# Expert blocks re-cut: rooms of 160 to 32 tokens by rank, 46 blocks of up to three experts, additions without the empty places, further blocks tested in sevens

## What is computed

```python
scores = sigmoid(uf @ w_router)              # 512 tokens, 64 experts
choice = scores + router_bias
masked = where(expert in the 4 best of 8 groups, choice, -inf)
_, top_e = top_k(masked, 8)                  # 8 experts of each token: 4096 rows in all
wts = scores[top_e] / sum(scores[top_e]) * 2.5
for each expert e:                           # D_MODEL 1024, D_EXPERT 256
    hid = silu(xb @ we_gate[e]) * (xb @ we_up[e])     # xb: the tokens that chose e
    routed[token] += (hid @ we_down[e]) * weight
shared = (silu(uf @ ws_gate) * (uf @ ws_up)) @ ws_down
return routed + shared
```

## Time and profile before

| what | value |
|---|---|
| time, median of 3 runs | 3088.01 us (3082.47 to 3090.04) |
| profiled execution: its own time | 3083.99 us |
| profiled execution: span of the core | 3082.7 us |
| PE busy | 2765.7 us, 90% of the span |
| DVE / ACT / POOL busy | 35% / 23% / 5% |
| TensorE clock granted, mean | 0.951 of full |
| DMA moved | 434.28 MB, mean 141 GB/s |

### The profile page before, as it was taken

One profiled execution on the slowest core, in us unless ns is written; L12 is line 12 of the kernel. 1 busy time (PEld: TensorE's weight loads), 2 busy tenths in 40 slices (PEclk: granted clock), 3 DMA queues, 4 the chain that ended last, 5 costly groups with the idle time before them and its releaser, 6 DMA issues.

```text
span 3082.7 us, 40644 instructions
## 1 busy us (share of the span) xinstructions
PE 2765.7 (90%) x16440; PEld 1663.5 (54%) x16440; DVE 1076.4 (35%) x2331; ACT 718.6 (23%) x1176; POOL 164.6 (5%) x132
## 2 busy tenths in 40 slices
PE   5999997999989799999999479979996988999797
PEld 2666663444437566677676234427875433555443
DVE  7666664322212122222222131016774113333312
ACT  2333331100021111111111020134553212333311
POOL 0000000000000122222222000000000000000000
PEclk8999998999998899999999789989998999999899
DMA  6222111333313598999999513221111211111110
GB/s 238 107 85 82 69 65 44 123 136 123 136 59 138 195 332 286 386 376 374 373 368 362 166 48 121 79 109 41 44 48 48 101 68 36 55 55 55 34 41 27
DMA packets 79045, 434.28 MB, mean 141 GB/s; under 512 B 11888, under 2 KB 12272, under 8 KB 36240
## 3 DMA queue, kind: packets, MB, share of 16 engines
q1 hardware_dynamic: 53296, 366.37, 30.7%
q0 software_dynamic: 15872, 46.16, 6.4%
q10 hardware_dynamic: 9696, 19.18, 1.7%
HBM read 395.95 MB, written 46.20 MB: 143 GB/s over the span
## 4 chain that ended last, share of the span: by engine, by line
PE 78%; DVE 8%; DMA 7%; ACT 5%; issue 2%; SPq 0%; DVEq 0%; POOL 0%; ACTq 0%; POOLq 0%
PE psum_all L274 34%; PE psum_all L1411 10%; PE psum_all L1853 7%; PE psum_all L1458 5%; DMA weights<-t_experts 4%; PE psum_all L3247 4%; PE psum_all L2000 4%; PE psum_all L3120 3%; PE psum_all L284 3%; PE psum_all L299 1%; PE psum_all L629 1%; DVE big L3381 1%; DVE h L3168 1%; DMA h<-x_t 1%; DMA total_rows<-big,rows 1%
## 5 line engine op out<-in xcount | busy, mean ns | idle before, releaser
L274 PE MATMUL psum_all<-u,weights 128*128 128x512 f32 x1024 | 449.8, 596 | 12.2 <-issue 12.2
L274 PE MATMUL psum_all<-big,weights 128*128 128x512 f32 (+1 forms) x768 | 338.1, 595 | 6.7 <-DVE big L3413 4.2
L274 PEld LDWEIGHTS psum_all<-u,weights 128*128 128x128 f32 x1024 | 193.8, 191 | 246.1 <-issue 245.7
L1411 PE MATMUL psum_all<-big 128*128 128x256 f32 (+1 forms) x1280 | 261.5, 383 | 15.4 <-ACT big L1390 15.4
L274 PEld LDWEIGHTS psum_all<-big,weights 128*128 128x128 f32 (+1 forms) x768 | 144.5, 189 | 194.4 <-issue 187.8
L1411 PEld LDWEIGHTS psum_all<-big 128*128 128x128 f32 (+1 forms) x1280 | 210.7, 180 | 53.6 <-ACT big L1390 16.0
L1853 PE MATMUL psum_all<-big,weights 128*128 128x512 f32 x512 | 222.3, 597 | 14.0 <-DVE big L1923 14.0
L1853 PEld LDWEIGHTS psum_all<-big,weights 128*128 128x128 f32 x512 | 98.1, 192 | 138.2 <-issue 134.2
L274 PE MATMUL psum_all<-weights,u 128*128 128x256 f32 (+1 forms) x704 | 153.5, 383 | 9.6 <-ACT u L412 9.6
L274 PEld LDWEIGHTS psum_all<-weights,u 128*128 128x128 f32 x704 | 135.2, 203 | 30.3 <-ACT u L412 10.4
L284 PE MATMUL psum_all<-const_cols,big 128*128 128x128 f32 (+2 forms) x952 | 133.3, 280 | 18.6 <-DVE big L789 11.0
(11 more groups left out here) (346 smaller groups left out, 3394.8 us busy)
## 6 DMA issues: line engine op xcount, KB each, us to landing
big<-t_experts SPq DMA_DIRECT2D x96, 1024.0 KB, 23.2
weights<-t_experts SPq DMA_DIRECT2D x96, 1024.0 KB, 18.0
weights<-t_ada SPq DMA_DIRECT2D x24, 1024.0 KB, 7.0
weights<-t_rkvg SPq DMA_DIRECT2D x16, 1024.0 KB, 5.5
rwkv_inputs<-big ACTq DMA_DIRECT2D x48, 256.0 KB, 2.0
big<-rwkv_inputs SPq DMA_DIRECT2D x8, 1280.0 KB, 6.8
weights<-t_x SPq DMA_DIRECT2D x8, 1024.0 KB, 4.9
weights<-t_BC SPq DMA_DIRECT2D x8, 1024.0 KB, 4.9
```

What stands on the lines that cost most here:

```text
L274: last = pe.matmul(out, lhsT, rhs, start=n == 0, stop=n == len(terms) - 1)
L1411: ins = pe.matmul(K.psum[rows, bank, n * F_E:(n + 1) * F_E], xT[:, k, rows], X.part(r, n, KD, F_E)[:, k, :], start=k == 0, stop=k == KD - 1)
```

## The change

**Rooms and blocks.** Rooms are now 160 (ranks 0 to 7), 128 (8 to 23), 96 (24 to 31), 64 (32 to 55) and 32 (56 to 63), which is enough for the counts given above. The 46 blocks are of four kinds: 24 `alone` (one expert, 128 places), 10 `two` (64 and 64), 8 `most` (96 places of one of the ranks 24 to 31 and 32 of one of 56 to 63) and 4 `more` (places 128 to 159 of two of the ranks 0 to 7, 32 partitions each, and 64 places of one of 32 to 35). `ORDER`, the order of the loads, follows from the first use of each rank.

**Matmuls.** `shares` cuts a part of 96 places into 64 and 32, so `most` and `more` blocks take three matmuls for each column of weights where a block of two took two. The list of a block comes from one group of matmuls, without the second one of two columns.

**Additions.** Each part of a block has an addition of its own, over all 128 places, in which the places outside the part and the empty ones carry a number over 511 and are left out. There are 24 + 10 x 2 + 8 x 2 + 4 x 3 = 72 additions; before there were 32 + 20 x 2 = 72. Real rows are 4096; before, 32 x 128 + 40 x 64 = 6656 rows were added, 2560 of them to spare rows.

**Start.** The shared output goes to four buffers of its own, in the room of u, so no copy waits for a store, and POOL issues the stores ahead of most gathers.

**Further blocks.** The loop is nested: five tests, and only if one holds, seven turns behind it.

```diff
+ROOM = [160] * 8 + [128] * 16 + [96] * 8 + [64] * 24 + [32] * 8
+SPANS = ((0, 128), (0, 96), (96, 128), (0, 64), (64, 128), (0, 32), (32, 64))
...
-    put("spare_row", T + r + 0 * c[:, 0:2])
+    put("spare_row", np.concatenate([T + np.where((r >= a) & (r < b), r, 4 * T) for a, b in SPANS], 1))
...
-    for j in range(16):
-        yield (2 * j,), 0
-        yield (2 * j + 1,), 0
-        if 2 * j < WITH_MORE:
-            yield (2 * j, 2 * j + 1), P
-        yield (ALONE + 2 * j, ALONE + 2 * j + 1), 0
+    alone = lambda r: [(r, 0, 0, 128)]
+    two = lambda r, s: [(r, 0, 0, 64), (s, 0, 64, 128)]
+    most = lambda r, s: [(r, 0, 0, 96), (s, 0, 96, 128)]
+    more = lambda r, s, t: [(r, 128, 0, 32), (s, 128, 32, 64), (t, 0, 64, 128)]
+    for j in range(4):
+        yield from (alone(2 * j), alone(2 * j + 1), more(2 * j, 2 * j + 1, 32 + j))
+        yield from (most(24 + 2 * j, 56 + 2 * j), alone(8 + 4 * j), two(36 + 5 * j, 37 + 5 * j), alone(9 + 4 * j))
+        yield from (most(25 + 2 * j, 57 + 2 * j), alone(10 + 4 * j), two(38 + 5 * j, 39 + 5 * j), alone(11 + 4 * j))
+        if j % 2:
+            yield two(35 + 5 * j, 40 + 5 * j)
...
-    ins = products(pe, K.psum[:, 7, 0:4], [(X.sel[n][:, t, :], X.rhs[n][:, t, :]) for t in range(NT)])
-    if two:
-        ins = products(pe, K.psum[0:HEAD, 7, 4:6], [(X.sel[n][:, t, HEAD:P], X.rhs[n][:, t, 0:2]) for t in range(NT)])
-    ins.then_inc(*q.pe.tick("list", b))
+    products(pe, K.psum[:, 7, 0:m], [(X.sel[n][:, t, :], X.rhs[n][:, t, 0:m]) for t in range(NT)]).then_inc(*q.pe.tick("list", b))
...
+    for r, _, start, end in BLOCKS[b]:
+        if end - start == 96:
+            yield r, slice(start, start + 64)
+            yield r, slice(start + 64, end)
+        else:
+            yield r, slice(start, end)
...
-    if len(BLOCKS[e][0]) == 1:
-        pool.indirect_dma_start(K.total_rows, bass.IndirectOffsetOnAxis(ap=rows[:, 1:2], axis=0), y, None,
-                                compute_op=ALU.add).then_inc(*K.added.tick(e))
-        return
...
+    if len(parts) > 1:
+        pool.wait_ge(*q.dve.at("add lists", e))
+    for i in range(len(parts)):
+        n = 1 if len(parts) == 1 else 2 + i
+        pool.indirect_dma_start(K.total_rows, bass.IndirectOffsetOnAxis(ap=rows[:, n:n + 1], axis=0), y, None,
+                                bounds_check=T - 1, oob_is_err=False, compute_op=ALU.add) \
+            .then_inc(*(K.added.tick(e) if i == len(parts) - 1 else K.added.tick(e, i)))
+        if i < len(parts) - 1:
+            pool.wait_ge(*K.added.at(e, i))
...
-            if t >= 2 and half == 0:
-                act.wait_ge(*K.shared_stored[t % 2].at(t - 2))
-            act.activation(X.y[t % 2][:, half * 512:half * 512 + 512], K.psum[:, 2 * (t % 2) + half, :], ACT.Copy) \
+            act.activation(X.shared_y[t][:, half * 512:half * 512 + 512], K.psum[:, 2 * (t % 2) + half, :], ACT.Copy) \
...
-    with nc.Fori(0, EXTRA) as i:
-        with nc.If(i < limit):
+    with nc.Fori(0, EXTRA, SEVEN) as first:
+        with nc.If(first < limit):
+            with nc.Fori(0, SEVEN) as n:
+                i = first + n
```

More of the change, by code:

```diff
@@ L1047, in __init__ @@
         self.sel = [K.carve(NT, P) for _ in range(2)]
-        self.rhs = [K.carve(NT, 4) for _ in range(2)]
+        self.rhs = [K.carve(NT, 6) for _ in range(2)]
         self.info = [K.carve(8) for _ in range(self.TURN)]
@@ L1056, in __init__ @@
         self.y = [K.carve(D) for _ in range(2)]
+        self.shared_y = [K.u[:, 2 * t:2 * t + 2, :].rearrange("p a b -> p (a b)") for t in range(NT)]
         self.ring = [K.carve(2048) for _ in range(6)] + [slot[:, :] for slot in K.W.slots]
@@ L1317, in select_dve @@
 def select_dve(K, X, q, b):
-    dve, n, (ranks, first) = K.nc.vector, b % 2, BLOCKS[b]
-    m = P // len(ranks)
+    dve, n, parts = K.nc.vector, b % 2, BLOCKS[b]
     if b >= 2:
@@ L1347, in list_dve @@
     dve.wait_ge(*q.pe.at("list", b))
[L1348 removed]
+    dve.tensor_copy(info[:, 0:2 + len(parts)], K.psum[:, 7, 0:2 + len(parts)]).then_inc(*q.dve.tick("rows", b))
     dve.wait_ge(*q.dve.now())
     dve.scalar_tensor_tensor(info[:, 6:7], info[:, 1:2], X.minus, info[:, 0:1], ALU.mult, ALU.add).then_inc(*q.dve.tick())
[L1351 to L1354 removed]
+    for i, (_, _, start, end) in enumerate(parts[1:]):
+        dve.tensor_copy(info[start:end, 2:3], info[start:end, 3 + i:4 + i]).then_inc(*q.dve.tick())
     dve.wait_ge(*q.dve.now())
[L1356 to L1358 removed]
+    dve.tensor_tensor(rows[:, 1:2], info[:, 6:7], K.c("spare_row")[:, 0:1], ALU.add).then_inc(*q.dve.tick("gather list", b))
+    if len(parts) > 1:
+        for i, (_, _, start, end) in enumerate(parts):
+            n = SPANS.index((start, end))
+            dve.tensor_tensor(rows[:, 2 + i:3 + i], info[:, 6:7], K.c("spare_row")[:, n:n + 1], ALU.add) \
+                .then_inc(*(q.dve.tick("add lists", b) if i == len(parts) - 1 else q.dve.tick()))
 def gather_pool(K, X, q, b):
@@ L1367, in gather_pool @@
         pool.wait_ge(*q.pe.at("turn", b - X.AHEAD, 1))
-    pool.wait_ge(*q.dve.at("listed", b))
+    pool.wait_ge(*q.dve.at("gather list", b))
     pool.indirect_dma_start(X.x_rows[b % X.AHEAD], None, K.u_rows,
@@ L1483, in add_pool @@
 def add_pool(K, X, q, e):
-    pool = K.nc.gpsimd
+    pool, y, rows, parts = K.nc.gpsimd, X.y[e % 2], K.rows[e % X.TURN], BLOCKS[e]
     if e:
@@ L3601, in build_program @@
     K.u_stored, K.added = K.new_signal("u_stored"), K.new_signal("rows_added")
-    K.shared_stored = [K.new_signal(f"shared_stored{n}") for n in range(2)]
+    K.shared_stored = K.new_signal("shared_stored")
     K.gathered = [K.new_signal(f"gathered{n}") for n in range(Moe.AHEAD)]
@@ L3611, in build_program @@
     K.expert_in = [K.new_signal(f"expert_in{n}") for n in range(Moe.RING)]
-    K.rows = [K.sb(f"rows{n}", [P, 3], I32) for n in range(Moe.TURN)]
+    K.rows = [K.sb(f"rows{n}", [P, 5], I32) for n in range(Moe.TURN)]
     K.number = K.sb("numbers", [P, 2 + E_ALL], I32)
```

66 lines of the change are left out of this document (23 added, 43 removed).

## The result

The changed kernel takes 3202.5 us (median of 4 runs, 3195.66 to 3206.07), the kernel before 3086.47 us on the same chip: a ratio of 1.0376, 95% interval 1.0361 to 1.039. The forecast was 3065 us with a range of 3036 to 3095, so the change cost 116 us where it was to gain some 20. The profiled execution has a span of 3204.8 us.

A forecast was written before the change was run, and what follows sets the result against it. PE, the loads and the chain of additions were taken to be at their limit together. From 3084.0 us, 20 less for loads, 12 more for additions and 12.5 less for the loop gave 3063.5, raised to 3065; range 3036 to 3095.

The forecast's parts named there:

- the part on PE: PE's products: 46 rounds of 12.57 us instead of 52 of about 13, 98 us less; three-part blocks at price 0.
- two at a time: Gate and up of three-part blocks: if parts overlapped only so, 3.6 us more in 12 blocks, 43 us; 0 was taken.
- the three-part blocks at 10 us and more: Gate and up of `most` and `more` blocks: a sign that the forecast is wrong; it expected 7.1 us.
- The start: First gate product: some 1008.4 instead of 1021.7 us, 13.2 us earlier; the loads decide what of it lasts.
- The loop: Tests after the last addition: 26 fewer save 12.5 us, 14.4 at most, at 0.48 us each.
- The bytes: Additions on q0: 2560 empty places dropped save 10.5 MB, and a load falls from 3.39 to 3.3 us.
- The price of 10.2 us: Chain of additions: a part naming 128 places lasts between a half, 9.05, and a full one, 10.9 us.
- the factor of 0.90: Chain of additions: faster with the DMA less full, so 751 us become 676, ending at 1711 us.
- rival 2: Chain of additions binds behind each `more` block, over 9.9 us a mean addition: 3097 us, half-way 3080; chance 33%.
- they will hold each other up: Chains of loads and additions, of one length: 3 us for each of four groups of five additions, 12 us charged.
- The ring's holes: Loads: the full ring leaves the DMA idle 14.6 or 12.5 us ahead of down of blocks 13, 25 and 36.

The follow-up runs named there:

- experiment 1: The changed kernel with every part of its three-part blocks cut in tiles of 32 places: 3086.96 us, ratio 1.0007 to before.
- experiment 2: The changed kernel with the same tiles issued sorted by width, all steps of one width and then all of the other: 3157.01 us, one run.
- experiment 6: The kernel before with the changed start, the nested loop and additions that leave out empty places over their own 64 places: 3053.12 us, ratio 0.9898.
- experiment 5: The kernel before with additions that leave out empty places alone, halves still over their own 64 places: 3077.88 us, ratio 0.9976.
- experiment 9: Experiment 1 with each part's addition over its own places alone, from a list of its own: 3057.45 us.
- experiment 13: Experiment 9 with the block of three experts moved between the blocks of its two big experts: 3032.01 us, ratio 0.9818.
- experiment 3: The changed kernel with the rooms and 52 blocks of before, each part's addition still over 128 places: 3079.0 us, ratio 0.9982.
- experiment 12: Experiment 6 with bounds_check=0 on every addition, so each is issued and waited for but only row 0 is added: 3026.49 us.

## Why the prediction was wrong

**The step that failed** is in the part on PE: "If the three parts only overlapped two at a time, it is half of 7.1 us more, 3.6 in 12 blocks, 43 us, mostly under the loads. I take 0." The price was 11.0 us for gate and up and 4.4 for down, 185 us in all. Both ends of its bound were wrong. The row that I leaned on, 36 ns for each of 3072 tiles, has one width only; it spoke for the issue rate and said nothing of tiles of unlike widths side by side. Down was given no price of its own. The bound of two at a time assumed that a 64 and a 32 overlap. The runs show that here only tiles of one width do (experiments 1 and 2: 64 slots where one width needs 32) and that each change of width costs 0.13 us.

The Trainium skill (TensorEngine Tiling (Array Packing), "Key Properties") says that changing the tiling mode drains the engine. The trace agrees, and the order of the instructions, 64, 32, 32, 64, 32, 32, was on view ahead of the run. The page gives no price; had its rule been weighed, 31 changes in the gate and up of a block would at least have been a rival with a chance of its own. The prediction's own sign for this, "the three-part blocks at 10 us and more", is what came.

**The start** was right: 13.2 us forecast, the gate product 11.8 us earlier in the trace, and 14.4 us left for it by subtraction in experiment 6. It lasted there, where the loads were thought to decide.

**The loop** was right in kind: 12.5 forecast, 10.3 measured alone; the pause fell from 17.2 to 3.4 us in the trace. So 26 tests took 0.40 to 0.53 us each, near the row's 0.48.

**The bytes** were right, 10.45 MB. Their worth was taken too high: 0.09 us off each of 178 loads is 16 us, and alone on the kernel before they gave 7.3 us (experiment 5).

**The additions' form.** This was the second step that failed, hidden under the first. The price of 10.2 us for a part over 128 places was fair: the six additions in a row above start 10.4 us apart in the mean. But the factor of 0.90, by which 72 additions were to take 676 us, was not. In experiment 1 they take 711.6 us from the first issue (1032.98) to the last landing (1744.59), 9.9 us each, just the mean at which rival 2 was to decide, and near its 723 us; its time, 3080 to 3097, has the measured 3087 in the middle. Of the forecast and this rival, the rival was thus the true one beneath the failed step: "they will hold each other up" was charged with 12 us, and own places (experiment 9) brought 29.5.

**The ring's holes** were right in place: the changed kernel has them at blocks 13, 25 and 36, as named. Their cause is borne out by experiment 13, where moving the three-part block between its experts gave 25 us. The three holes as sized in the prediction come to 42 us; the additions, which bind again in that run, may have taken back the rest, which no run separates.

**The account.** The prediction's PE time with 185 us more makes 46 x 12.57 + 185 = 763 us, from 1010 on to 1773. With the 68 us in which PE is idle in the four windows above it is 1841 of the 1858.6 seen. The other 18 us are PE's own: it is busy 781.0 of the 850 us from 1010 to 1860, at a granted clock of 0.95, and the gate products that come behind a wait are longer (20.85 us at 1139.96 and 19.65 us at 1553.89 in place of 18.12). The gains of the start and the loop are in these numbers, covered by the loss. The additions and the holes are in the change as well, but mostly beside a busy PE. They come to cost 29.5 and 25 us once its blocks are mended.

**Left open:** why an added byte costs the DMA engines twice a loaded one; what of the 26 us between experiments 3 and 6 is the left-out places' packets and what the other way of making the lists; what the second buffer costs besides the 5 us of reading it; and what still holds experiment 13, since no run there takes the additions' bytes away.

## What to carry to other kernels

Before packing narrow matmuls beside one another, write down the widths in the order in which they are issued: tiles of one width overlapped up to fourfold here at no cost, and one unlike tile in each step made gate and up 2.5 times as long. Cut the wide part into the narrow width rather than leave it whole. When a change removes work from one of several chains of equal length, cost the others in the new form too (here a list that names 128 places for 32 rows), and order the blocks by when they give back what the loads wait for, not only by what they need.

## What the hardware showed that I had not expected

- 128 records of 32 columns, four tiles side by side, took 7.08 us, 64 of 64 columns, two side by side, 7.1 us, and a mixture of 96 took 18.12 us in turn and 14.38 us sorted.
- An addition by row numbers costs the DMA engines 5.1 us a MB against 2.5 for a load in the same stretch (experiments 6 and 12).
- A place that an addition leaves out by its number still takes a packet: 18432 packets with 2560 such places more, 15872 without them, at the same 35.7 MB (experiments 3 and 6).
- An addition with half or more of its places out of bounds is not cheap as a wait: the kernel with 40 parts over 128 places is 26 us slower than with 64 (experiments 3 and 6, which differ in their lists too), and own places brought 29.5 us (experiment 9).
